# Two query heads at a time in the second block's grouped attention

## The chip, the cores and the metric

The kernel runs on one core of a Trainium2 chip. The core has five engines that run side by side and wait for one another by semaphores: TensorE (PE) for matmuls and transposes, VectorE (DVE), ScalarE (ACT), GpSimd (POOL) and SyncE (SP), which here only issues transfers from HBM. The metric is the time of one execution in microseconds (us) on the device. The time before is 2065.9 us, the median of 3 runs (2061.59 to 2067.75).

## The reference, cut to what matters

Two layers of a first block work on 256 tokens of width 1024, then comes a second block: a projection, two kinds of attention, an output projection, and a mixture of 32 experts. The change touches only the grouped attention (GQA) in the second block: 8 query heads of 64, 2 key/value heads, 256 queries against 512 keys (256 of a context, 256 of the tokens).

```python
def gqa_attention(q, k, v, q_block):          # q [1,256,8,64], k and v [1,512,2,64], q_block 128
    def block(qi):
        s = jnp.einsum('bhgqd,bkhd->bhgqk', qi, k) * scale
        p = jax.nn.softmax(s, axis=-1)
        return jnp.einsum('bhgqk,bkhd->bqhgd', p, v)
...
        lat_mix = jnp.concatenate([
            gqa_attention(qa, ka_all, va_all, Q_BLOCK),
            diff_attention(qb, kb_all, vb_all, lam, diff_subln[l], lambda_init, Q_BLOCK),
        ], axis=-1)
        x = x + gt1 * (lat_mix @ w_o[l])
        x = x + gt2 * moe_ffn(...)
```

The differential attention after it has 4 heads, each with two score matrices whose softmaxes are subtracted, and values of width 128.

## The kernel before

**Where the work stands.** The two layers take about the first 850 us, the second block's projections and attention some 190 us, routing about 75 us, the experts the rest. In the attention a list of jobs is worked through: `BJOBS` holds 16 GQA jobs, one for each query head and each tile of 128 queries, and then 8 differential jobs. Each engine's program is written out by hand as a loop over `j`, one step for each job plus one, and the engines meet only at semaphores, so a step of one engine can lie beside another step of another.

**A step on PE** (lines 759 to 775). `scores(j)` multiplies queries and keys of job j into the PSUM tile `score` (128 x 1024, two banks). A GQA job uses only one half of it, the halves in turn (`half_of`). Heads have 64 rows, so the matmul uses 64 of the array's 128 rows (line 726); `qaT` holds an even head in partitions 0 to 63 and an odd one in 64 to 127, and `kaT` holds each key head twice, in both halves. Then `values(j-1)`: four transposes of the probabilities into the one PSUM tile `flip` (line 741), half a projection unit of the later stages as filling (`bfill`, lines 691 and 644), and the product with the values, four blocks of 128 keys, into 64 partitions of `mixed` (line 751). Every matmul in plain fp32 is two MATMUL records in the trace; a transpose is one. After that, where a projection unit that needs turning is complete, `turn(u)` transposes it, through the same `flip` (line 701).

**What is filled in.** The units of `BUNITS` from number 6 on are the projections qb (2), kb (4), vb (4) and four pieces of `ada`; `BHALVES` says how many halves each step computes: four in step 0, then one in each of the 24 steps. `BDONE_IN[s]` lists the units that are complete in step s; DVE or ACT takes them out of their bank there or one step on, and qb and kb are turned in the next step.

**ACT** (lines 1029 to 1052) in step j copies `flip` of job j-1 to `turned` (line 1034), then computes the exponentials of job j from `score` to `probs`, with their sum (lines 1042 and 1045), and then evacuates units and turned units (line 1021). **DVE** (lines 1231 to 1266) takes the maximum of the scores of job j (line 1238 for GQA, 1241 for differential), evacuates the units of the step before (line 1216 and the rotation at 1175 to 1181), divides by the sum (lines 1250 and 1251), and copies `mixed` of job j-1 to `mix` (line 1264). `score_left` gives the count that PE waits for before it writes `score`: in the GQA jobs that of the job before the last one, since the halves alternate; otherwise that of the last.

**SP** issues the weights in the order of their list. A ring slot is written when the last unit that reads it is complete, so the expert tiles that follow wait for the last of the `ada` pieces and for the output projection (lines 579 to 621). From the second expert on, each tile's load waits until PE has used the same tile of the expert before (lines 600 to 611).

Of the kernel before, what the change touches and what calls it, by code (L numbers as in the profile page):

```python
# [20 lines left out]
ALU = mybir.AluOpType  # L21
ACT = mybir.ActivationFunctionType
AX = mybir.AxisListType

P = 128
# [140 lines left out]
BJOBS = [("gqa", h, t) for h in range(AHEADS) for t in range(TT)]  # L166
# [3 lines left out]
BHALVES = [4] + [1] * NBJ  # L170
# [5 lines left out]
for s_ in range(1, NBJ + 1):  # L176
    BFLIPS.append(("job", s_ - 1))
    BFLIPS += [("turn", u) for u in BDONE_IN[s_ - 1] if u in BTURNED]
# [34 lines left out]
def build(nc, c_in, xT, ctxT, consts, layer_params, block_params, w_in, w_uq, w_ukv, w_out_a, w_out_b, w_out_c,  # L213
          w_o, w_ada, w_qkv, w_o2, e_in, eb_in, e_out, eb_out, out, sizes=None, debug=None):
    PER = sizes or CHAINED
    with ExitStack() as ctx:
# [351 lines left out]
        def half_of(j):  # L568
            return j % 2 if BJOBS[j][0] == "gqa" else 0

# [84 lines left out]
        def block_tensor(pe):  # L655
# [63 lines left out]
            def scores(j):  # L719
                kind, hd, t = BJOBS[j]  # L720
                pe.wait_ge(score_free, score_left(S_JOBS + j))
                cols = slice(t * P, (t + 1) * P)
                if kind == "gqa":
                    lo = HALF * (hd % 2)
                    o = score[:, W * half_of(j):W * half_of(j) + W]
                    ins = pe.matmul(o, qaT[lo:lo + HALF, hd // 2, cols], kaT[lo:lo + HALF, hd // 4, :],  # L726
                                    start=True, stop=True)
                else:
                    for cp in range(2):
                        lo = HALF * cp  # L730
                        ins = pe.matmul(score[:, W * cp:W * cp + W], qbT[lo:lo + HALF, hd, cols],
                                        kbT[lo:lo + HALF, hd, :], start=True, stop=True)
                ins.then_inc(scored, 1)

            def values(j):
                kind, hd, t = BJOBS[j]
                pe.wait_ge(bprobs, j + 1)
                f = FLIP0 + BFLIPS.index(("job", j))
                pe.wait_ge(flip_free, f + 1)
                for i in range(4):  # L740
                    ins = pe.transpose(flip[:, i * P:(i + 1) * P], probs[:, j % 2, i * P:(i + 1) * P], ident)
                ins.then_inc(flipped, 1)
                bfill()
                pe.wait_ge(flip_free, f + 2)
                pe.wait_ge(mixed_free, MIXED0 + j + 1)
                for i in range(4):
                    pt = turned[:, j % 2, i * P:(i + 1) * P]
                    if kind == "gqa":
                        lo = HALF * (hd % 2)
                        kv = hd // 4  # L750
                        ins = pe.matmul(mixed[lo:lo + HALF, 0:P], va[:, i, kv * HALF:(kv + 1) * HALF], pt,  # L751
                                        start=i == 0, stop=i == 3)
                    else:
                        ins = pe.matmul(mixed[:, 0:P], vb[:, i, hd * P:(hd + 1) * P], pt, start=i == 0, stop=i == 3)
                ins.then_inc(mixed_done, 1)
# [3 lines left out]
            for j in range(NBJ + 1):  # L759
                if j < NBJ:  # L760
                    if j == 2 * AHEADS:
# [4 lines left out]
                if j == 2 * AHEADS + 1:  # L766
# [215 lines left out]
        def block_scalar(act):  # L982
# [46 lines left out]
            for j in range(NBJ + 1):  # L1029
                if j > 0:  # L1030
                    act.wait_ge(flipped, FLIP0 + BFLIPS.index(("job", j - 1)) + 1)
                    if j >= 3:
                        act.wait_ge(mixed_done, MIXED0 + j - 2)
                    act.activation(turned[:, (j - 1) % 2, :], flip[:, :], ACT.Copy).then_inc(flip_free, 1)
                if j < NBJ:
                    kind = BJOBS[j][0]
                    act.wait_ge(bmasked, j + 1)
                    if j >= 2:
                        act.wait_ge(flipped, FLIP0 + BFLIPS.index(("job", j - 2)) + 1)
                    st = stat[:, j % 2, :]  # L1040
                    a = W * half_of(j)
                    ins = act.activation(probs[:, j % 2, 0:W], score[:, a:a + W], ACT.Exp, bias=st[:, 2:3],
                                         accum_out=st[:, 4:5])
                    if kind == "diff":
                        ins = act.activation(probs[:, j % 2, W:2 * W], score[:, W:2 * W], ACT.Exp, bias=st[:, 3:4],
                                             accum_out=st[:, 5:6])
                    ins.then_inc(score_free, 1)
# [67 lines left out]
        def block_vector(dve, link, steps, base):  # L1115
# [115 lines left out]
            for j in range(NBJ + 1):  # L1231
                if j < NBJ:
# [3 lines left out]
                    a = W * half_of(j)  # L1236
                    if kind == "gqa":
                        link(dve.tensor_reduce(st[:, 0:1], score[:, a:a + W], AX.X, ALU.max))
                        dve.tensor_scalar(st[:, 2:3], st[:, 0:1], -1.0, None, ALU.mult).then_inc(bmasked, 1)
                    else:  # L1240
                        link(dve.tensor_reduce(st[:, 0:2], score[:, :].rearrange("p (a n) -> p a n", a=2), AX.X, ALU.max))
                        dve.tensor_scalar(st[:, 2:4], st[:, 0:2], -1.0, None, ALU.mult).then_inc(bmasked, 1)
                for u in BDONE_IN[j - 1] if j else ():
                    evacuate_block(u)
                if j < NBJ:
                    kind, hd, t = BJOBS[j]
                    pr, st = probs[:, j % 2, :], stat[:, j % 2, :]
                    dve.wait_ge(score_free, SCORE0 + S_JOBS + j + 2)
                    if kind == "gqa":
                        link(dve.reciprocal(st[:, 6:7], st[:, 4:5]))  # L1250
                        dve.tensor_scalar(pr[:, 0:W], pr[:, 0:W], st[:, 6:7], None, ALU.mult).then_inc(bprobs, 1)
                    else:
                        link(dve.reciprocal(st[:, 6:8], st[:, 4:6]))
# [4 lines left out]
                if j > 0:  # L1258
                    kind, hd, t = BJOBS[j - 1]
                    lo = HALF * (hd % 2)  # L1260
                    dve.wait_ge(mixed_done, MIXED0 + j)
                    cols = slice(t * P, (t + 1) * P)
                    if kind == "gqa":
                        dve.tensor_copy(mix[lo:lo + HALF, hd // 2, cols], mixed[lo:lo + HALF, 0:P]).then_inc(mixed_free, 1)
                    else:
                        dve.tensor_copy(mix[:, 4 + hd, cols], mixed[:, 0:P]).then_inc(mixed_free, 1)
# [1121 lines left out]
```

## Time and profile before

| what | us |
|---|---|
| median of 3 runs | 2065.9 |
| profiled execution, its own time | 2067.96 |
| profiled execution, span of the trace | 2066.1 |
| PE busy | 1931.6 (93%) |
| DVE busy / ACT busy | 766.3 / 547.8 |
| share of DMA and of PE in the chain that ended last | 32% / 57% |
| from the scores of job 1 to the end of the values of job 15 | 890.15 to 997.18 |
| the differential steps after it, to the start of the last transposes | 997.18 to 1031.33 |
| first matmul of the experts | 1116.52 |

The span is what the trace covers; the device adds 1.9 us around it. Busy shares are means over stages with different limits. The GQA stage is one where PE has no gap, the differential stage one where PE waits in each step, and the experts one where the transfers run at full rate. What the change touches must be read from the GQA stage alone.

### The profile page before, as it was taken

The numbers are of one execution on the slowest core, as the hardware profiler recorded it, in microseconds if no ns is written. First come the engines' busy times: TensorE is split into PE (matmuls) and PEld (weight loads), VectorE is DVE, ScalarE is ACT, GpSimd is POOL, SyncE is SP. The second block draws the span as 40 slices with busy tenths as digits, with TensorE's granted clock in tenths as the row PEclk, the third lists the DMA queues.
The fourth block names the chain that finished last, engine by engine and source line by source line (L and its number), as shares of the span: only waits on it lengthen the run. The fifth ranks groups of instructions, "written<-read, shape, count | busy, mean of one in ns | idle before, by whom it ended". The sixth has DMA issues, their size and how long they took to land.

```text
span 2066.1 us, 26980 instructions
## 1 busy us (share of the span) xinstructions
PE 1931.6 (93%) x10970; PEld 1215.5 (59%) x10970; DVE 766.3 (37%) x1477; ACT 547.8 (27%) x922; POOL 522.2 (25%) x220
## 2 busy tenths in 40 slices
PE   7999999989999999899888999999999999999996
PEld 6779889977798899444465344333333334333333
DVE  4784643348737533734544111111111111111112
ACT  4554455445544554112411000000000000000001
POOL 5775655767665566000000000000000000000000
PEclk9999999999999999899987999999999999999998
DMA  8554333565543335311542999999999999999994
GB/s 294 203 184 164 123 123 123 186 219 195 174 164 141 111 135 206 128 41 41 204 170 121 419 428 429 428 429 429 428 429 428 429 428 428 429 428 429 428 429 179
DMA packets 111408, 563.21 MB, mean 273 GB/s; under 512 B 4768, under 2 KB 24352, under 8 KB 86464
## 3 DMA queue, kind: packets, MB, share of 16 engines
q1 hardware_dynamic: 111328, 562.09, 68.1%
q8 instruction: 57, 0.93, 0.2%
q14 instruction: 23, 0.19, 0.0%
HBM read 561.02 MB, written 1.05 MB: 272 GB/s over the span
## 4 chain that ended last, share of the span: by engine, by line
PE 57%; DMA 32%; DVE 8%; ACT 2%; issue 1%; SPq 0%; DVEq 0%; ACTq 0%
DMA ring<-in_e_in_dram 32%; PE bank L1605 14%; PE bank L1595 10%; PE score L868 9%; PE bank L691 4%; PE bank L1572 3%; PE mixed L903 2%; PE bank L801 1%; PE mixed L1689 1%; PE flip L1672 1%; DVE ring L2174 1%; PE score L726 1%; PE score L1658 1%; PE flip L1630 1%; PE mixed L751 1%
## 5 line engine op out<-in xcount | busy, mean ns | idle before, releaser
L1981 POOL TENSOR_TENSOR w_lo<-ring,w_hi 128x1024 fp32r<-128x1024 f32 (+1 forms) x216 | 522.0, 2427 | 289.2 <-ACT w_hi L1883 288.4
L868 PE MATMUL score<-ring,space 128*64 128x512 f32 x2048 | 461.6, 595 | 46.8 <-DMA ring<-in_e_in_dram 45.8
L868 PEld LDWEIGHTS score<-ring,space 128*64 128x64 f32 x2048 | 142.3, 137 | 354.8 <-issue 245.6
L1883 ACT ACTIVATE w_hi<-ring 128x1024 fp32r<-128x1024 f32 (+1 forms) x216 | 226.4, 1049 | 222.6 <-PE bank L1605 123.6
L1605 PE MATMUL bank<-h_hi,w_hi 128*128 128x256 f32 x896 | 262.3, 293 | 0.0
L1605 PE MATMUL bank<-h_lo,w_hi 128*128 128x256 f32 x896 | 254.7, 284 | 0.0
L1605 PE MATMUL bank<-h_hi,w_lo 128*128 128x256 f32 x896 | 254.5, 284 | 0.0
L903 PE MATMUL mixed<-ring,space 128*64 128x512 f32 x1024 | 226.8, 595 | 0.0
L1084 ACT ACTIVATE space<-space 128x512 f32<-128x512 f32 x32 | 20.2, 631 | 719.7 <-DVE space L1385 719.7
L1385 DVE TENSOR_SCALAR space<-score 128x512 f32<-128x512 f32 x32 | 22.2, 694 | 432.7 <-PE score L868 432.7
L1605 PEld LDWEIGHTS bank<-h_hi,w_hi 128*128 128x128 f32 x896 | 173.3, 193 | 4.5 <-issue 4.4
L1605 PEld LDWEIGHTS bank<-h_lo,w_hi 128*128 128x128 f32 x896 | 173.1, 193 | 0.1
L1605 PEld LDWEIGHTS bank<-h_hi,w_lo 128*128 128x128 f32 x896 | 172.8, 193 | 0.0
L903 PEld LDWEIGHTS mixed<-ring,space 128*64 128x64 f32 x1024 | 70.7, 137 | 132.6 <-issue 130.6
L1595 PE MATMUL bank<-w_hi,h_hi 128*128 128x512 f32 (+1 forms) x320 | 131.3, 410 | 8.5 <-DVE h_lo L2037 8.5
L1398 DVE COPY space<-mixed 64x512 f32<-64x512 f32 x32 | 21.9, 684 | 295.6 <-PE mixed L903 295.6
L1595 PE MATMUL bank<-w_hi,h_lo 128*128 128x512 f32 (+1 forms) x320 | 125.1, 391 | 0.0
L1595 PE MATMUL bank<-w_lo,h_hi 128*128 128x512 f32 (+1 forms) x320 | 124.6, 390 | 0.0
L1595 PEld LDWEIGHTS bank<-w_hi,h_hi 128*128 128x128 f32 x320 | 61.1, 191 | 25.9 <-issue 12.8
L691 PE MATMUL bank<-ring,h 128*128 128x512 f32 (+1 forms) x160 | 68.4, 582 | 5.1 <-DVE h L1149 5.1
L1595 PEld LDWEIGHTS bank<-w_hi,h_lo 128*128 128x128 f32 x320 | 60.9, 190 | 12.0
L1595 PEld LDWEIGHTS bank<-w_lo,h_hi 128*128 128x128 f32 x320 | 61.1, 191 | 11.7 <-issue 1.0
(329 smaller groups left out, 2378.0 us busy)
## 6 DMA issues: line engine op xcount, KB each, us to landing
ring<-in_e_in_dram SPq DMA_DIRECT2D x128, 2048.0 KB, 25.2
ring<-in_e_out_dram SPq DMA_DIRECT2D x64, 2048.0 KB, 22.1
ring<-in_w_in_dram SPq DMA_DIRECT2D x42, 2048.0 KB, 7.8
ring<-in_w_ada_dram SPq DMA_DIRECT2D x16, 1024.0 KB, 5.3
ring<-in_w_o_dram SPq DMA_DIRECT2D x6, 2048.0 KB, 8.2
ring<-in_w_qkv_dram SPq DMA_DIRECT2D x4, 2048.0 KB, 10.1
ring<-in_w_ada_dram SPq DMA_DIRECT2D x4, 2048.0 KB, 8.0
ring<-in_w_out_a_dram SPq DMA_DIRECT2D x2, 2048.0 KB, 7.7
```

The lines of the kernel that those rows point to most:

```text
L691: ins = pe.matmul(b[:, 0:n], src[:, c, tt * P:(tt + 1) * P], w8[:, c, 0:n], start=c == 0, stop=c == DC - 1)
L726: ins = pe.matmul(o, qaT[lo:lo + HALF, hd // 2, cols], kaT[lo:lo + HALF, hd // 4, :], start=True, stop=True)
L751: ins = pe.matmul(mixed[lo:lo + HALF, 0:P], va[:, i, kv * HALF:(kv + 1) * HALF], pt, start=i == 0, stop=i == 3)
L868: ins = pe.matmul(score[HALF * blk:HALF * blk + HALF, which * W:(which + 1) * W], xs[:, 2 * j + r, HALF * hh:HALF * hh + HALF], wk[:, blk ...
L903: ins = pe.matmul(mixed[HALF * side:HALF * side + HALF, :], actT[:, hh, a * P + HALF * half:a * P + HALF * half + HALF], ring[:, 4 + half, ...
L1385: dve.tensor_scalar(glu[:, hh, :], score[:, 0:W], GLU_LIMIT, None, ALU.min).then_inc(glu_free, 1)
L1398: dve.tensor_copy(ys[0:HALF, hh, :], mixed[0:HALF, :])
L1572: ins = pe.matmul(b[:, i * T:(i + 1) * T], w_[:, c, m], y_[br][:, c, :], start=c == 0 and i == 0 and y_ is y_hi and w_ is hi, stop=c == 3 ...
L1595: ins = pe.matmul(b[:, 0:n], x_[:, c, t], w_[:, k % PARTS, i, 0:n], start=c == 0 and x_ is h_hi and w_ is w_hi, stop=c == DC - 1 and x_ is ...
L1605: ins = pe.matmul(b[:, half * T:(half + 1) * T], w_[:, k % PARTS, i, m:m + P], x_[:, c, :], start=c == 0 and half == 0 and x_ is h_hi and ...
L1883: act.activation(split_part(w_hi, k), raw_part(k), ACT.Copy).then_inc(hi_done, 1)
L1981: pool.tensor_tensor(split_part(w_lo, k), raw_part(k), split_part(w_hi, k), ALU.subtract).then_inc(lo_done, 1)
```

## The change

A GQA job now holds two neighbouring query heads. `BJOBS` has 8 GQA jobs (head pair, query tile) in place of 16. Their scores are written by two matmuls, one in each row half of the array, to the two halves of `score`. Their 8 blocks of probabilities go through `flip` in two rounds of four, in each of which the heads alternate (`BROUNDS`); each round has its own filling, so a GQA step computes two halves of units (`BHALVES`). The values of the two heads go to the two partition halves of `mixed` in turns, and one copy of 128 partitions takes them out. Since both halves of `score` are in use, PE waits for the exponentials of the job just before. The differential jobs are as they were.

```diff
-BJOBS = [("gqa", h, t) for h in range(AHEADS) for t in range(TT)]
+BJOBS = [("gqa", h, t) for h in range(0, AHEADS, 2) for t in range(TT)]
+NGQA = len(BJOBS)
...
-BHALVES = [4] + [1] * NBJ
+BROUNDS = [[[(w, c) for c in (2 * r, 2 * r + 1) for w in range(2)] for r in range(2)] if job[0] == "gqa" else
+           [[(0, c) for c in range(4)]] for job in BJOBS]
+BHALVES = [4] + [2] * NGQA + [1] * (NBJ - NGQA)
...
         def score_left(s):
-            s1 = s - S_JOBS
-            alone = not 1 <= s1 < 2 * AHEADS
-            return SCORE0 + s + (1 if alone else 0)
+            return SCORE0 + s + 1
...
-                if kind == "gqa":
-                    lo = HALF * (hd % 2)
-                    o = score[:, W * half_of(j):W * half_of(j) + W]
-                    ins = pe.matmul(o, qaT[lo:lo + HALF, hd // 2, cols], kaT[lo:lo + HALF, hd // 4, :],
-                                    start=True, stop=True)
+                for w in range(2):
+                    rows = slice(HALF * w, HALF * w + HALF)
+                    if kind == "gqa":
+                        q, k = qaT[rows, hd // 2, cols], kaT[rows, hd // 4, :]
...
+                    ins = pe.matmul(score[:, W * w:W * w + W], q, k, start=True, stop=True)
...
+                pe.wait_ge(mixed_free, MIXED0 + j + 1)
+                for r, blocks in enumerate(BROUNDS[j]):
+                    pe.wait_ge(flip_free, job_flip(j, r) + 1)
+                    for i, (w, c) in enumerate(blocks):
+                        ins = pe.transpose(flip[:, i * P:(i + 1) * P], probs[:, j % 2, w * W + c * P:w * W + (c + 1) * P],
+                                           ident)
+                    ins.then_inc(flipped, 1)
+                    bfill()
+                    pe.wait_ge(flip_free, job_flip(j, r) + 2)
+                    pt = turned[:, (BFIRST_ROUND[j] + r) % 2, :]
+                    for i, (w, c) in enumerate(blocks):
+                        if kind == "gqa":
+                            kv = hd // 4
+                            o, v = mixed[HALF * w:HALF * w + HALF, 0:P], va[:, c, kv * HALF:(kv + 1) * HALF]
+                        else:
+                            o, v = mixed[:, 0:P], vb[:, c, hd * P:(hd + 1) * P]
+                        ins = pe.matmul(o, v, pt[:, i * P:(i + 1) * P], start=c == 0, stop=c == 3)
...
                 if j > 0:
-                    act.wait_ge(flipped, FLIP0 + BFLIPS.index(("job", j - 1)) + 1)
-                    if j >= 3:
-                        act.wait_ge(mixed_done, MIXED0 + j - 2)
-                    act.activation(turned[:, (j - 1) % 2, :], flip[:, :], ACT.Copy).then_inc(flip_free, 1)
+                    if j >= 2:
+                        act.wait_ge(mixed_done, MIXED0 + j - 1)
+                    for r in range(len(BROUNDS[j - 1])):
+                        act.wait_ge(flipped, job_flip(j - 1, r) + 1)
+                        act.activation(turned[:, (BFIRST_ROUND[j - 1] + r) % 2, :], flip[:, :], ACT.Copy
+                                       ).then_inc(flip_free, 1)
...
+                    for w in range(2):
+                        ins = act.activation(probs[:, j % 2, w * W:(w + 1) * W], score[:, w * W:(w + 1) * W], ACT.Exp,
+                                             bias=st[:, 2 + w:3 + w], accum_out=st[:, 4 + w:5 + w])
...
+                    link(dve.reciprocal(st[:, 6:8], st[:, 4:6]))
                     if kind == "gqa":
-                        link(dve.reciprocal(st[:, 6:7], st[:, 4:5]))
-                        dve.tensor_scalar(pr[:, 0:W], pr[:, 0:W], st[:, 6:7], None, ALU.mult).then_inc(bprobs, 1)
+                        dve.tensor_scalar(pr[:, 0:W], pr[:, 0:W], st[:, 6:7], None, ALU.mult)
+                        dve.tensor_scalar(pr[:, W:2 * W], pr[:, W:2 * W], st[:, 7:8], None, ALU.mult).then_inc(bprobs, 1)
...
-                        dve.tensor_copy(mix[lo:lo + HALF, hd // 2, cols], mixed[lo:lo + HALF, 0:P]).then_inc(mixed_free, 1)
+                    dve.tensor_copy(mix[:, at, t * P:(t + 1) * P], mixed[:, 0:P]).then_inc(mixed_free, 1)
```

On PE, two steps of the program before (scores, transposes, half a unit of filling, values, each twice; the first has the turning of a kb unit behind it) stand as follows. A row with x3 is the rest of four.

```order
L726 MATMUL score<-space 128x512 [waits score_free]
L741 MATMUL flip<-cst,space 128x128 [waits flip_free,bprobs]
L741 MATMUL flip<-cst,space 128x128 x3
L691 MATMUL bank<-ring,space 128x512 [waits bank_free1,landed3]
L691 MATMUL bank<-ring,space 128x512 x3
L751 MATMUL mixed<-space 64x128 [waits mixed_free,flip_free]
L751 MATMUL mixed<-space 64x128 x3
L701 MATMUL flip<-cst,space 128x128 [waits flip_free,bqn_ready]
L701 MATMUL flip<-cst,space 128x128 x3
L726 MATMUL score<-space 128x512 [waits score_free]
```

One step of the changed program does the work of two: a second score matmul, then two rounds.

```order
L733 MATMUL score<-space 128x512 [waits score_free]
L733 MATMUL score<-space 128x512
L743 MATMUL flip<-cst,space 128x128 [waits flip_free,mixed_free,bprobs]
L743 MATMUL flip<-cst,space 128x128 x3
L695 MATMUL bank<-ring,space 128x512 [waits bank_free1,landed3]
L695 MATMUL bank<-ring,space 128x512 x3
L755 MATMUL mixed<-space 64x128 [waits flip_free]
L755 MATMUL mixed<-space 64x128 x3
L743 MATMUL flip<-cst,space 128x128 [waits flip_free]
L743 MATMUL flip<-cst,space 128x128 x3
L695 MATMUL bank<-ring,space 128x512 x4
L755 MATMUL mixed<-space 64x128 [waits flip_free]
```

The wait for `mixed_free` has moved from the values to the transposes ahead of them, and the two score matmuls stand side by side. On ACT, in the same part of the program before, each copy of `flip` (line 1034) is followed by the exponentials of one head.

```order
L1034 ACTIVATE space<-flip 128x512 [waits mixed_done,flipped]
L1042 ACTIVATE space<-score,space 128x512 [waits flipped,bmasked]
L1034 ACTIVATE space<-flip 128x512 [waits mixed_done,flipped]
L1042 ACTIVATE space<-score,space 128x512 [waits flipped,bmasked]
L1021 ACTIVATE space<-flip 128x4x128 [waits flipped]
```

In the changed program ACT has both copies of `flip` first, then both heads' exponentials.

```order
L1036 ACTIVATE space<-flip 128x512 [waits flipped,mixed_done]
L1036 ACTIVATE space<-flip 128x512 [waits flipped]
L1044 ACTIVATE space<-score,space 128x512 [waits flipped,bmasked]
L1044 ACTIVATE space<-score,space 128x512
L1022 ACTIVATE space<-flip 128x4x128 [waits flipped]
```

So the exponentials of job j have moved behind the second copy of job j-1.

## Rows read from the trace of the kernel before

**Rows 1.** Busy time by stretch: us, engines (instructions), granted PE clock, DMA share, GB/s.

```profile
890.15:901.00 10.85, 7.79 (x32) 4.10 (x31) 8.77 (x31) 1.87 (x4) 0.00 (x0) 0.92 0.56 193
901.00:909.51 8.51, 8.51 (x23) 4.03 (x22) 1.50 (x4) 1.87 (x4) 0.00 (x0) 0.70 0.00 0
909.51:991.08 81.57, 81.57 (x303) 40.31 (x303) 31.38 (x93) 20.68 (x46) 0.00 (x0) 1.00 0.08 27
997.18:1031.33 34.15, 27.02 (x169) 12.92 (x169) 21.68 (x50) 15.79 (x38) 0.00 (x0) 1.00 0.82 308
```

**Rows 2.** Timeline, PE, a GQA step: start, us, line, operation.

```profile
960.61 1.12 PE L726 MATMUL score<-space 64*128 64x512 f32 x2
961.67 0.66 PE L741 MATMUL flip<-cst,space 128*128 128x128 f32 x4
962.16 3.60 PE L691 MATMUL bank<-ring,space 128*128 128x512 f32 x8
965.69 1.09 PE L751 MATMUL mixed<-space 128*64 128x128 f32 x8
966.71 1.12 PE L726 MATMUL score<-space 64*128 64x512 f32 x2
```

**Rows 3.** Timeline, PE, first differential scores.

```profile
991.08 1.13 PE L731 MATMUL score<-space 64*128 64x512 f32 x4
992.14 0.66 PE L741 MATMUL flip<-cst,space 128*128 128x128 f32 x4
```

**Rows 4.** Timeline, PE, layer attention: values, then transposes.

```profile
352.08 0.66 PE L1689 MATMUL mixed<-space 128*64 128x128 f32 x8
352.67 0.66 PE L1672 MATMUL flip<-cst,space 128*128 128x128 f32 x4
```

**Rows 5.** Timeline, PE, steps 1 and 2.

```profile
896.24 0.66 PE L701 MATMUL flip<-cst,space 128*128 128x128 f32 x4
899.96 1.11 PE L701 MATMUL flip<-cst,space 128*128 128x128 f32 x4 [3.06 <-DVEq L1227]
901.00 2.07 PE L726 MATMUL score<-space 64*128 64x512 f32 x2
```

**Rows 6.** Timeline, PE, a later step with a turned unit.

```profile
915.62 0.65 PE L701 MATMUL flip<-cst,space 128*128 128x128 f32 x4
916.20 1.12 PE L726 MATMUL score<-space 64*128 64x512 f32 x2
```

**Rows 7.** Timeline, DVE and ACT, in step 1 (qb1 begins with the copy at 896.09).

```profile
891.31 0.69 DVE L1238 TENSOR_REDUCE space<-score 128x1 f32<-128x512 f32 x1 [15.01 <-PE score L726]
896.09 0.69 DVE L1216 COPY space<-bank 128x512 f32<-128x512 f32 x1 [0.23 <-DVE space L1181]
896.93 0.60 ACT L1021 ACTIVATE space<-flip 128x512 f32<-128x512 f32 x1 [3.77 <-PE flip L701]
899.99 0.16 DVE L1250 RECIPROCAL space<-space 128x1 f32<-128x1 f32 x1 [0.15 <-DVE space L1181]
900.19 0.49 DVE L1251 TENSOR_SCALAR space<-space 128x512 f32<-128x512 f32 x1
```

**Rows 8.** Timeline, all engines, a differential step.

```profile
998.36 1.23 DVE L1241 TENSOR_REDUCE space<-score 128x2 f32<-128x1024 f32 x1 [0.78 <-PE score L731]
999.82 0.69 ACT L1042 ACTIVATE space<-score,space 128x512 f32<-128x512 f32 x1 [0.29 <-DVE space L1242]
1001.30 0.17 DVE L1253 RECIPROCAL space<-space 128x2 f32<-128x2 f32 x1 [1.52 <-ACT space L1045]
1002.89 0.28 DVE L1266 COPY space<-mixed 128x128 f32<-128x128 f32 x1
1003.02 0.66 PE L741 MATMUL flip<-cst,space 128*128 128x128 f32 x4 [0.57 <-DVE space L1256]
```

**Rows 9.** Busy time by stretch, the end of the routing.

```profile
1100.00:1116.00 16.00, 14.28 (x52) 11.55 (x52) 14.01 (x37) 1.02 (x2) 0.00 (x0) 0.55 0.00 1
```

**Rows 10.** Timeline, SP, loads of expert tiles.

```profile
1120.42 12.34 SPq L598 DMA_DIRECT2D ring<-in_e_in_dram  x4
```

More of the change, by code:

```diff
@@ L165 @@
 AHEADS, DIFFS = 8, 4
-BJOBS = [("gqa", h, t) for h in range(AHEADS) for t in range(TT)]
+BJOBS = [("gqa", h, t) for h in range(0, AHEADS, 2) for t in range(TT)]
+NGQA = len(BJOBS)
 BJOBS += [("diff", h, t) for h in range(DIFFS) for t in range(TT)]
 NBJ = len(BJOBS)
-BHALVES = [4] + [1] * NBJ
+BROUNDS = [[[(w, c) for c in (2 * r, 2 * r + 1) for w in range(2)] for r in range(2)] if job[0] == "gqa" else
+           [[(0, c) for c in range(4)]] for job in BJOBS]
+BFIRST_ROUND = [sum(map(len, BROUNDS[:j])) for j in range(NBJ + 1)]
+BHALVES = [4] + [2] * NGQA + [1] * (NBJ - NGQA)
+assert all(BHALVES[j + 1] >= len(BROUNDS[j]) for j in range(NBJ))
 assert sum(BHALVES) == 2 * (BQKV - BFIRST)
@@ L176 @@
 for s_ in range(1, NBJ + 1):
-    BFLIPS.append(("job", s_ - 1))
+    BFLIPS += [("job", s_ - 1, r) for r in range(len(BROUNDS[s_ - 1]))]
     BFLIPS += [("turn", u) for u in BDONE_IN[s_ - 1] if u in BTURNED]
@@ L562, in score_left, with job_flip @@
         def score_left(s):
-            s1 = s - S_JOBS
-            alone = not 1 <= s1 < 2 * AHEADS
-            return SCORE0 + s + (1 if alone else 0)
-        def half_of(j):
-            return j % 2 if BJOBS[j][0] == "gqa" else 0
+            return SCORE0 + s + 1
+        def job_flip(j, r):
+            return FLIP0 + BFLIPS.index(("job", j, r))
         def block_sync(sp):
@@ L722, in scores @@
                 cols = slice(t * P, (t + 1) * P)
-                if kind == "gqa":
-                    lo = HALF * (hd % 2)
-                    o = score[:, W * half_of(j):W * half_of(j) + W]
-                    ins = pe.matmul(o, qaT[lo:lo + HALF, hd // 2, cols], kaT[lo:lo + HALF, hd // 4, :],
-                                    start=True, stop=True)
[L728 to L732, printed above, removed]
+                for w in range(2):
[3 more added lines that the diff above has]
+                    else:
+                        q, k = qbT[rows, hd, cols], kbT[rows, hd, :]
+                    ins = pe.matmul(score[:, W * w:W * w + W], q, k, start=True, stop=True)
                 ins.then_inc(scored, 1)
@@ L737, in values @@
                 pe.wait_ge(bprobs, j + 1)
[L738 to L744, printed above, removed]
-                pe.wait_ge(mixed_free, MIXED0 + j + 1)
[L746 to L754, printed above, removed]
+                pe.wait_ge(mixed_free, MIXED0 + j + 1)
+                for r, blocks in enumerate(BROUNDS[j]):
[11 more added lines that the diff above has]
+                            o, v = mixed[HALF * w:HALF * w + HALF, 0:P], va[:, c, kv * HALF:(kv + 1) * HALF]
+                        else:
+                            o, v = mixed[:, 0:P], vb[:, c, hd * P:(hd + 1) * P]
+                        ins = pe.matmul(o, v, pt[:, i * P:(i + 1) * P], start=c == 0, stop=c == 3)
                 ins.then_inc(mixed_done, 1)
@@ L765, in block_tensor @@
                     scores(j)
[L766 removed]
+                if j == NGQA + 1:
                     for u in range(BADA - 4, BADA):
@@ L1235, in block_vector @@
                     dve.wait_ge(scored, SCORE0 + S_JOBS + j + 1)
[L1236 to L1242, printed above, removed]
+                    link(dve.tensor_reduce(st[:, 0:2], score[:, :].rearrange("p (a n) -> p a n", a=2), AX.X, ALU.max))
+                    dve.tensor_scalar(st[:, 2:4], st[:, 0:2], -1.0, None, ALU.mult).then_inc(bmasked, 1)
                 for u in BDONE_IN[j - 1] if j else ():
@@ L1259, in block_vector @@
                     kind, hd, t = BJOBS[j - 1]
-                    lo = HALF * (hd % 2)
                     dve.wait_ge(mixed_done, MIXED0 + j)
-                    cols = slice(t * P, (t + 1) * P)
-                    if kind == "gqa":
-                        dve.tensor_copy(mix[lo:lo + HALF, hd // 2, cols], mixed[lo:lo + HALF, 0:P]).then_inc(mixed_free, 1)
-                    else:
-                        dve.tensor_copy(mix[:, 4 + hd, cols], mixed[:, 0:P]).then_inc(mixed_free, 1)
+                    at = hd // 2 if kind == "gqa" else 4 + hd
+                    dve.tensor_copy(mix[:, at, t * P:(t + 1) * P], mixed[:, 0:P]).then_inc(mixed_free, 1)
             dve.wait_ge(scored, SCORE0 + S_SUB + 1)
```

12 lines of the change are left out of this document (2 added, 10 removed).

## The prediction

> **What bounds the kernel now.** I read the busy time by stretch first. The attention starts with scores of job 1 at 890.15 and the last GQA values end at 997.18. In the long middle, 909.51 to 991.08, PE is busy for all of 81.57 us at a granted clock of 1.00, DVE for 31.4 and ACT for 20.7 [rows 1]. So in this stage only PE's work sets the time, and anything taken off PE shortens it until another engine is late. Next I read PE's timeline there, where starts and not durations count, since matmuls overlap. A step is 6.10 us from scores to scores: 1.06 for the scores of one head (two records), 0.49 for four transposes, 3.53 for half a unit of filling, 1.02 for the values (eight records) [rows 2]. A turned unit adds 0.58 [rows 6]. The chain of waits names the same four lines and nothing else in this stage.
>
> The stage begins worse. In step 1 PE waits 3.06 us for DVE, which has to rotate two qb units, and after that its clock is low: scores that take 1.12 elsewhere are recorded with 2.07, transposes 1.11 for 0.66 [rows 2, 5], and the granted clock is 0.70 from 901.00 to 909.51 [rows 1]. That stretch holds one plain step of 6.10 in 8.51, so 2.41 is lost to the clock, and the turning at 899.96 lasts 1.04 to the next start where it takes 0.58 [rows 5, 6], another 0.46. With the wait this is 5.93 us. Check: 16 steps of 6.10 and six turnings of 0.58 are 101.1, and with 5.93 give 107.0, which is 997.18 less 890.15.
>
> **The change on PE.** The number of blocks, of filling halves and of turnings is the same, so they cost what they did. Two things shrink.
> - Scores: 16 jobs of 1.06 become 8 jobs with two matmuls in two row halves. The differential jobs do just this, and four records take 1.06 from start to start [rows 3], no more than two records do [rows 2]. This saves 8 x 1.06 = 8.5 us.
> - Values: before, eight records in one column half take 1.02. In the layers' attention eight records of the same shape, which alternate between the column halves, take 0.59 to the next transposes [rows 4]. 16 such rounds save 16 x (1.02 - 0.59) = 6.9 us.
>
> A new step is then 1.06 + 2 x (0.49 + 3.53 + 0.59) = 10.28 us against 12.20 for two old ones.
>
> **Step 1.** Today PE reaches the turning of qb1 after one half of filling. Now it does two rounds first. From 890.15: scores to 891.21, first round to 895.82, second round to 900.43, turning of qb0 to 901.0. DVE has the same rotation, started 0.54 later, because it now reduces both heads (1.23 for 0.69) [rows 7, 8]; its qb1 took from 896.09 to 899.99 [rows 7], so it is ready at about 900.5, before PE asks. The 3.06 us wait goes. What is late next is the single `flip`: the second turning needs the first one copied. From the transposes at 896.24 to the end of ACT's copy at 896.93 + 0.60 are 1.29 [rows 5, 7]; with a small semaphore delay I take 1.35 in place of 0.58, a new gap of 0.8 us. As the gap is short, I let the clock stay high and give back the 2.41 and 0.46. Gain in step 1: 5.9 - 0.8 = 5.1 us. The bounds: if the clock falls all the same, only 3.06 - 0.8 = 2.3 is left; if PE also finds DVE late by as much as now, the new gap makes it -0.8; without any gap it is 5.9. I take 5.1, since the wait and the low clock stand next to each other in the rows.
>
> **Is another engine late then?** Per step, counted from the start of the scores: the second transposes start at 5.7; ACT copies `flip` from 6.4 to 7.0, then the exponentials of both heads, which with their sums take 1.5 in the differential jobs (999.82 to 1001.30) [rows 8], to 8.5. PE wants `score` at 10.3: 1.8 to spare. DVE divides with 0.2 + 2 x 0.5 [rows 7], to 9.8; PE wants the probabilities at 10.3 + 1.06: 1.5 to spare. The tightest is the copy of `mixed`, which the transposes now wait for: values end at 10.3, the copy of 0.28 [rows 8] is done at about 10.7, needed at 11.3. It lies beside the scores, with 0.6 to spare. Behind that wait stand filling and values, so if the copy were late, its whole lateness would be PE's. Rotating a kb unit (about 4 us on DVE) lies between the reduction, done at 2.6, and the division at 8.6. Cost of all of these: nothing, and at the other end 1.9 us a step if the wait should reach the whole saving, 15.3 us.
>
> **Downstream.** The differential steps are bound by DVE, ACT and PE in turn (period 4.7, PE waiting 0.57 for probabilities in each [rows 8]; granted clock 1.00 [rows 1]), not changed, and enter with the same work done. The units come earlier, never later, in relation to the loads: the slots are freed earlier too. Routing needs the attention's result. In its last 16 us the transfers stand still (DMA share 0.00) [rows 9], since all six tiles are loaded, and the next expert load is issued at 1120.42, after the experts have begun [rows 10]. So the experts' stream of transfers, which bounds the rest, moves as a block with the attention's end.
>
> **Sum.** 8.5 + 6.9 + 5.1 = 20.5 us. The profiled execution took 2067.96 (span 2066.1 and 1.9 around it), so 2047.5; it lies 2.1 above the median of the three runs, and from the median it is 2045.4. I predict 2046.
>
> **Rivals.**
> - One pairing does not overlap. Then its term stays away: 8.5 (to 2054) or 6.9 (to 2052). For it: no row shows a GQA job with either pattern. Against: both patterns are in the trace, with the same shapes [rows 3, 4], the scores in two banks in each case. The Trainium skill, "TensorEngine Tiling (Array Packing)", Gotcha 1 (PSUM Pressure), says that different row tiles can't use one PSUM bank at the same time; were that so for column tiles, which do share the bank of `mixed`, the values would be the pairing that fails. The trace disagrees: 0.59 in one bank of `mixed` [rows 4].
> - ACT's order takes the saving back. The exponentials of job j now stand behind the second copy of job j-1, and `score` has no second half to write meanwhile. If PE waits about 1.9 us per step, 15.3 are gone and only step 1's 5.1 is left: 2061. Against it stands the 1.8 us to spare above. The skill's same page, section "PSUM Bottleneck", says that tiling quickens TensorE and not the evacuation of PSUM, which may then bound. By that rule this is where it would show; the trace agrees for the differential steps, where PE waits 0.57 [rows 8].
> - Slower: the same chain wholly exposed. From the reduction at 998.36 to the transposes at 1003.02 the differential chain takes 4.66 us [rows 8], in which PE would stand still once in each of the 8 new steps, because ACT reaches the exponentials only after the last filling of the step: 8 x 4.7 = 37, less 20.5, gives +17, or 2083. It decides for slower from 20.5 / 8 = 2.6 us of waiting per step on. It would need the copies and exponentials to come 4.4 us later than I count (1.8 to spare and 2.6). A low clock would add to it, as after the 3.06 us wait.
> - It is hidden. If the experts' transfers had been waiting for something that the attention does not move, the time stays at 2066. Against: the share of 0.00 [rows 9] and the load after the start [rows 10].
> - Better than I say: routing runs at a granted clock of 0.55 in its last 16 us [rows 9], and where the clock falls may move with the work's phase, by some 3 us either way; the good side is about 2041.
>
> **Chances.** Forecast 0.76; one pairing fails 0.10; better 0.04: these are faster, 0.90. ACT's order 0.04 and hidden 0.03 lie within 0.3% (6.2 us, about what a measurement of this kernel can tell from no change): 0.07. Slower 0.03. The forecast's own range is 2042 to 2051, from the clock (3 us) and from the runs' scatter. The range for 8 in 10 reaches up into the failed pairing: 2040 to 2055.
>
> **What would show it.** In the new trace, the four score records and the next transposes stand 1.06 apart; the values take 0.59 to what follows; a step is 10.3 us; PE has no gap in GQA steps beyond one of about 0.8 before the turning of qb1, where the clock stays at 1.00; the time from the scores of job 1 to the end of the last GQA values falls from 107.0 to about 86.6; from there to the first expert matmul it stays at 119.3 within 3 us. I am wrong if score records follow each other at 0.5 us (row halves one after the other), if PE waits for exponentials or for the copy of `mixed`, if the clock is low in that stage, or if the stage shrinks and the end does not.

## The result

| | median us | runs | ratio to the kernel before |
|---|---|---|---|
| before | 2065.4 | 4 (2061.6 to 2067.8) | |
| changed | 2038.2 | 4 (2036.6 to 2042.4) | 0.9873 (0.9852 to 0.9894) |
| predicted | 2046 | range 2040 to 2055 | |

The kernel became 27.2 us faster, 1.8 us below the low end of the range. In a second comparison the gain was 23.6 us (2062.7 to 2039.1, ratio 0.9881, 0.9864 to 0.9897). The predicted 20.5 us is right for the stage that was worked out, and too small for the whole.

Busy time by stretch in the changed kernel's first trace: job 0, then everything between the stage and the experts, then the experts. Columns are as in [rows 1].

```profile
867.84:884.48 16.64, 16.64 (x36) 6.73 (x36) 2.44 (x5) 2.70 (x5) 0.00 (x0) 0.90 0.11 40
971.07:1088.93 117.86, 93.19 (x469) 65.69 (x467) 64.19 (x143) 30.23 (x58) 0.00 (x0) 0.87 0.43 164
1088.93:2036.20 947.27, 884.43 (x4320) 368.31 (x4320) 170.08 (x368) 72.33 (x118) 0.00 (x0) 1.00 0.97 413
```

The same three stretches in the first trace of the kernel before:

```profile
871.77:890.15 18.38, 18.38 (x35) 7.44 (x35) 1.50 (x4) 2.03 (x3) 0.00 (x0) 0.81 0.09 32
997.18:1116.52 119.34, 95.09 (x467) 66.61 (x467) 64.34 (x144) 30.47 (x57) 0.00 (x0) 0.86 0.42 162
1116.52:2066.10 949.58, 885.82 (x4320) 369.18 (x4320) 169.88 (x368) 72.39 (x118) 0.00 (x0) 0.99 0.97 412
```

Span by span the 29.9 us between the two traces (2066.1 and 2036.2) come out as follows. Ahead of job 0's scores 3.9 (871.77 against 867.84); job 0 itself 1.7; the GQA stage 20.4 (107.03 against 86.59, the time from 884.48 to 971.07); behind it 1.5; the experts 2.3. Only the third of these numbers, the stage, was in the prediction's sum.

Inside the stage the rows are those that it named. These are lines from the timeline of one new step of the changed kernel, those that answer to [rows 2, 3, 4 and 8]; the weight loads and some shorter operations of ACT and DVE are left out. Line numbers are those of the changed kernel: 733 is the scores, 743 the transposes, 755 the values, 705 the turning.

```profile
907.63 1.13 PE L733 MATMUL score<-space 64*128 64x512 f32 x4
908.69 0.66 PE L743 MATMUL flip<-cst,space 128*128 128x128 f32 x4
909.18 3.60 PE L695 MATMUL bank<-ring,h 128*128 128x512 f32 x8
912.71 0.66 PE L755 MATMUL mixed<-space 128*64 128x128 f32 x8
913.30 0.66 PE L743 MATMUL flip<-cst,space 128*128 128x128 f32 x4
913.79 3.60 PE L695 MATMUL bank<-ring,h 128*128 128x512 f32 x8
913.99 0.60 ACT L1036 ACTIVATE space<-flip 128x512 f32<-128x512 f32 x1 [3.95 <-PE flip L743]
915.15 0.69 ACT L1044 ACTIVATE space<-score,space 128x512 f32<-128x512 f32 x1
916.56 0.48 DVE L1246 TENSOR_SCALAR space<-space 128x512 f32<-128x512 f32 x1
917.32 0.66 PE L755 MATMUL mixed<-space 128*64 128x128 f32 x8
918.02 0.29 DVE L1256 COPY space<-mixed 128x128 f32<-128x128 f32 x1 [0.98 <-PE mixed L755]
```

The four score records and the next transposes are 1.06 apart, the values take 0.59 to what follows, PE has no gap. Counted from the scores, ACT copies the second round at 6.4, has the second head's exponentials under way at 7.5, DVE ends at 9.4 and the copy of `mixed` at 10.7, 0.6 us ahead of the next transposes, which start at 11.3 or later. In step 1 PE's timeline answers to [rows 5]:

```profile
894.77 0.66 PE L705 MATMUL flip<-cst,space 128*128 128x128 f32 x4
896.21 0.63 PE L705 MATMUL flip<-cst,space 128*128 128x128 f32 x4 [0.78 <-ACT space L1022]
896.76 1.13 PE L733 MATMUL score<-space 64*128 64x512 f32 x4
```

The 3.06 us wait for DVE is now a 0.78 us wait for ACT's copy of `flip`, and the scores after it take 1.13 and not 2.07.

### The profile page after: what moved, and what is told of

It reads as the page before. It is cut to its first block, busy times and chain, and to the rows that moved or that the text cites. A ratio compares the mean times of both kernels' runs of the same rounds, so it can differ in the third digit from the quotient of the medians.

```text
span 2036.2 us, 26901 instructions
## 1 busy us (share of the span) xinstructions
PE 1904.2 (94%) x10970; PEld 1199.2 (59%) x10970; DVE 759.7 (37%) x1445; ACT 546.9 (27%) x922; POOL 522.6 (26%) x220
## 4 chain that ended last, share of the span: by engine, by line
PE 57%; DMA 31%; DVE 7%; ACT 2%; issue 1%; SPq 0%; DVEq 0%; ACTq 0%
DMA ring<-in_e_in_dram 31%; PE bank L1595 14%; PE bank L1585 10%; PE score L869 9%; PE bank L695 4%; PE bank L1562 3%; PE mixed L904 2%; PE bank L802 1%; PE mixed L1679 1%; PE flip L1662 1%; DVE ring L2164 1%; PE score L1648 1%; PE flip L1620 1%; PE bank L927 1%; PE score L887 1%
```

## The experiments

They answer two questions: whether the three terms inside the stage have the causes that I gave, and where the rest comes from. Since the stage is the same to 0.1 us from trace to trace, I read each from there; the whole time scatters by several microseconds.

**The two kernels once more** (nothing edited).

> The kernel before, unchanged, for a second trace. The changed kernel was 27.2 us faster, the attention stage only 20.4 us shorter. If the rest is chance (low-clock stretches that fall differently from run to run in parts that the change doesn't touch): the stage from the scores of job 1 to the end of the GQA values is again 107.0 within 0.5, while the start of that stage (890.15 in the first trace) moves by some us and the ratio to the kernel before is 1.000. If the rest is systematic: the stage starts again at 890 and the parts behind it take the same times as in the first trace.

> The changed kernel, unchanged. By chance: the stage is again 86.6 long, its start moves by some us from 884.5, and the gain over the kernel before in five rounds comes nearer to 20.4 than 27.2 is. Systematic: start again at 884.5, gain again 27.

Measured: the unchanged kernel before 2062.3, ratio to itself 0.9997 (0.9988 to 1.0007); the changed one 2039.1. Busy time by stretch, first the second trace of the kernel before, cut at the same events: ahead of job 0, job 0, the stage, behind it, the experts.

```profile
0.00:866.18 866.18, 822.59 (x5772) 716.77 (x5772) 487.11 (x828) 415.67 (x685) 523.09 (x220) 0.98 0.49 171
866.18:884.60 18.42, 18.42 (x34) 7.43 (x34) 1.50 (x4) 2.03 (x3) 0.00 (x0) 0.81 0.09 33
884.60:991.65 107.05, 104.00 (x379) 51.42 (x378) 44.91 (x135) 27.03 (x60) 0.00 (x0) 0.97 0.11 40
991.65:1111.00 119.35, 95.11 (x467) 66.66 (x467) 64.38 (x144) 30.44 (x57) 0.00 (x0) 0.86 0.42 162
1111.00:2060.70 949.70, 885.76 (x4320) 369.13 (x4320) 169.98 (x368) 72.38 (x118) 0.00 (x0) 0.99 0.97 412
```

And the second trace of the changed kernel:

```profile
0.00:871.73 871.73, 828.54 (x5772) 721.18 (x5773) 485.81 (x828) 415.66 (x685) 522.00 (x220) 0.97 0.49 170
871.73:888.44 16.71, 16.71 (x37) 6.86 (x37) 2.44 (x5) 2.69 (x5) 0.00 (x0) 0.89 0.10 36
888.44:975.02 86.58, 85.80 (x378) 40.85 (x377) 37.28 (x102) 26.14 (x58) 0.00 (x0) 1.00 0.14 49
975.02:1092.84 117.82, 93.16 (x469) 65.71 (x467) 64.17 (x143) 30.23 (x58) 0.00 (x0) 0.87 0.43 164
1092.84:2042.30 949.46, 885.84 (x4320) 369.18 (x4320) 170.15 (x368) 72.37 (x118) 0.00 (x0) 0.99 0.97 412
```

Neither theory holds whole. The part ahead of job 0 is chance: one and the same program reached job 0 at 871.77 and 866.18 in one kernel, at 867.84 and 871.73 in the other, and the first trace of the kernel before was the latest of them. So are the experts, 947.3 or 949.5 in the changed kernel. But two parts that I had counted as untouched are not chance: job 0 takes 18.4 in both traces of the kernel before and 16.6 to 16.7 in both of the changed one, at a granted clock of 0.81 against 0.89 and 0.90; and the part behind the stage takes 119.3 against 117.8. With the stage that is 1.7 + 20.4 + 1.5 = 23.6 us, the gain measured in this second comparison.

**Values in other orders and halves.** In `values_apart` the blocks of a round are sorted by head.

```diff
-BROUNDS = [[[(w, c) for c in (2 * r, 2 * r + 1) for w in range(2)] for r in range(2)]
+BROUNDS = [[[(w, c) for w in range(2) for c in (2 * r, 2 * r + 1)] for r in range(2)]
```

> The changed kernel with the blocks of a round sorted by head: two blocks in one column half, then two in the other, instead of in turns. If the saving of the values comes from two column halves at work side by side, eight records take about 1.02 again instead of 0.59 (perhaps 0.1 less, where the halves meet), the stage is 16 x 0.43 = 6.9 us longer, and the time 2045. If the saving comes from anything else in the fused job, the round stays at 0.59 and the time at 2038.

Measured: 2040.7, ratio 0.9898 (0.9876 to 0.9920), stage 86.7. The eight records still take 0.59 (PE's timeline):

```profile
911.54 0.66 PE L755 MATMUL mixed<-space 128*64 128x128 f32 x8
912.13 0.66 PE L743 MATMUL flip<-cst,space 128*128 128x128 f32 x4
```

So the turns, which I took for the reason, are not needed. In this order too the trace has two records under way from the first 0.02 us of a round on, as with the blocks in turns. Whether the halves are needed, `values_one_half` asks.

```diff
-o, v = mixed[HALF * w:HALF * w + HALF, 0:P], va[:, c, kv * HALF:(kv + 1) * HALF]
+o, v = mixed[0:HALF, 0:P], va[:, c, kv * HALF:(kv + 1) * HALF]
+first, last = (c == 0 and w == 0, c == 3 and w == 1) if kind == "gqa" else (c == 0, c == 3)
```

> The changed kernel with the values of both heads in the lower column half, summed into one result (the two heads are no longer kept apart). Sorting the blocks by head cost nothing, so either two column halves work side by side whatever the order of the records, or eight short records cost 0.59 here for another reason. Two halves needed: 1.02 per round, the stage 14 x 0.43 = 6.0 us longer and the whole 16 x 0.43 = 6.9 us. Another reason: 0.59, no change.

Measured: 2046.5, ratio 0.9914 (0.9896 to 0.9931). PE's timeline:

```profile
914.42 1.09 PE L756 MATMUL mixed<-space 128*64 128x128 f32 x8
915.44 0.66 PE L743 MATMUL flip<-cst,space 128*128 128x128 f32 x4
```

1.02 a round, as in the kernel before [rows 2], and the stage 93.47 for 86.58, which is 6.9. (All 16 rounds lie in the stage as I cut it; the 14 of the expectation was a slip.) The term of 6.9 is confirmed: two column halves work side by side, in both orders that were run.

**Scores in one row half** (`scores_one_half`).

```diff
-q, k = qaT[rows, hd // 2, cols], kaT[rows, hd // 4, :]
+q, k = qaT[0:HALF, hd // 2, cols], kaT[0:HALF, hd // 4, :]
```

> The changed kernel with both score matmuls of a GQA job in the lower row half (the second head's scores are left out, the first one's are computed twice). If the saving of the scores comes from two row halves at work side by side, four records take 1.06 + 0.86 = 1.9 instead of 1.06, the stage is 8 x 0.86 = 6.9 us longer, and the time 2045. If it comes from fewer changes between tile shapes, they stay near 1.06 and the time at 2038.

Measured: 2048.8, ratio 0.9934 (0.9918 to 0.9951). PE's timeline:

```profile
910.20 1.98 PE L733 MATMUL score<-space 64*128 64x512 f32 x4
912.12 0.66 PE L743 MATMUL flip<-cst,space 128*128 128x128 f32 x4
```

1.92 for 1.06; the stage, which holds seven of the eight GQA scores, is 92.53 for 86.58, 0.85 for each. The row halves carry this term. The whole time rose by 9.7 against the changed kernel's 2039.1, more than the 6.9 expected: job 0 took 19.26 for 16.7, and the part behind the stage 119.5 for 117.8. The granted clock is low for longer at both places; the next pair tests the first of them.

**Job 0's scores and the clock.** `before_job0_pair` adds a matmul to the kernel before:

```diff
+                    if j == 0:
+                        pe.matmul(mixed[:, :], qaT[HALF:P, 0, cols], kaT[HALF:P, 0, :], start=True, stop=True)
```

> The kernel before, with one more score matmul in job 0 alone: the odd head's, in the upper row half, into the tile mixed, where nobody reads it. In two traces of the kernel before, the time from the scores of job 0 to those of job 1 is 18.4 us, in three of the changed kernel and its variant with paired scores 16.6 to 16.8, though both fill the same four halves there. Theory: with both row halves at work in job 0's scores the clock comes back sooner, so this kernel takes 16.7 there and is 1.7 us faster than the kernel before. Rival: it is chance or the fused job's later work, and the stretch stays at 18.4.

`after_job0_single` changes job 0 of the changed kernel:

```diff
+                    if kind == "gqa" and j == 0:
+                        q, k = qaT[0:HALF, hd // 2, cols], kaT[0:HALF, hd // 4, :]
```

> The changed kernel, with both score matmuls of job 0 alone in the lower row half (the second head's scores of that job are left out, the first one's are computed twice). Theory (both row halves bring the clock back sooner): from job 0's scores to job 1's the low clock lasts longer, about 19.2 us instead of 16.7, the rest of the stage stays at 86.6. Rival: only the second matmul's own time is added, 0.9 us at the high clock or 1.7 at the low one, 17.6 to 18.4.

Measured: 2060.7 (ratio 0.9987, 0.9976 to 0.9999) and 2043.5 (0.9907, 0.9887 to 0.9928). Busy time by stretch, `before_job0_pair`, job 0 and the stage:

```profile
868.70:885.35 16.65, 16.65 (x37) 6.72 (x37) 1.50 (x4) 2.03 (x3) 0.00 (x0) 0.90 0.12 43
885.35:991.13 105.78, 102.72 (x380) 50.76 (x379) 44.90 (x135) 27.04 (x60) 0.00 (x0) 0.98 0.11 40
```

`after_job0_single`, job 0:

```profile
866.34:885.61 19.27, 19.27 (x36) 7.81 (x37) 2.44 (x5) 2.69 (x5) 0.00 (x0) 0.82 0.08 31
```

One more matmul makes the kernel before shorter by 1.7 us in job 0: granted clock 0.90 where it was 0.81. In the other direction job 0 takes 19.27, at 0.82, against the theory's 19.2 and at most 18.4 for the rival. That is 0.9 more than in the kernel before: a second matmul in the same row half costs its own time and does nothing for the clock. Job 0 comes after gaps in which PE waits for ACT and DVE (2.22, 0.70 and 0.48 us in the kernel before), and its clock is low there at the start. One rival is left: `before_job0_pair` came to job 0 with the clock still high (the two transposes ahead of it took 0.41), the kernel before with the clock already low (0.66). The second traces of the two kernels settle it, since both come to job 0 with the clock low. Their job 0 cut 3.60 and 7.00 us after the start of the scores, first the kernel before:

```profile
866.18:869.78 3.60, 3.60 (x4) 1.34 (x5) 0.85 (x2) 1.82 (x2) 0.00 (x0) 0.50 0.45 167
869.78:873.18 3.40, 3.40 (x5) 1.35 (x4) 0.65 (x2) 0.20 (x2) 0.00 (x0) 0.50 0.00 0
```

Then the changed kernel:

```profile
871.73:875.33 3.60, 3.60 (x6) 1.34 (x7) 1.40 (x2) 1.26 (x2) 0.00 (x0) 0.50 0.45 166
875.33:878.73 3.40, 3.40 (x9) 1.52 (x8) 1.05 (x3) 1.43 (x4) 0.00 (x0) 1.00 0.00 0
```

With paired scores the full clock is back 3.6 us after they start, with single ones 7.0 us after; 3.4 us at half the clock cost 1.7 us, the whole difference. The other traces fall in the same two groups: 3.6 us wherever the scores of job 0 are paired, `before_job0_pair` too, and 7.0 us in `scores_one_half`, `after_job0_single` and `before_no_rotation`. That paired scores bring the clock back sooner is thus shown in both directions, for this place. The stage of `before_job0_pair` is also 1.3 shorter than 107.05, with the low clock around the 3.06 us wait shorter (the scores there are recorded with 1.52 and not 2.07); this I had not expected. The two together are the 3.0 us between the medians, 2063.7 and 2060.7, of which the interval of the ratio only just excludes nothing.

The 1.5 us behind the stage need no pairing to appear. Eleven traces, in which PE has the same instructions there, give 117.8 (the changed kernel twice, `values_apart`, `values_one_half`, and below `fill_behind` and `before_no_rotation`, which has no pairing), 119.3 to 119.5 (the kernel before twice, `before_job0_pair`, `scores_one_half`) and 121.8 (`after_job0_single`). The kernel before shows a low clock around the last differential step. PE's timeline in its second trace, whose first row follows a wait of 1.98:

```profile
1025.79 0.66 PE L741 MATMUL flip<-cst,space 128*128 128x128 f32 x4 [1.98 <-DVE space L1256]
1026.38 1.55 PE L644 MATMUL bank<-ring,silu 128*32 128x512 f32 x8
1027.86 2.08 PE L754 MATMUL mixed<-space 128*128 128x128 f32 x8
```

In the changed kernel the wait before the same transposes is 2.00, and the filling and values after it take 1.07 and 1.16:

```profile
1005.46 0.63 PE L743 MATMUL flip<-cst,space 128*128 128x128 f32 x4 [2.00 <-DVE space L1250]
1006.01 1.07 PE L648 MATMUL bank<-ring,silu 128*32 128x512 f32 x8
1007.01 1.16 PE L755 MATMUL mixed<-space 128*128 128x128 f32 x8
```

The same wait, once with the clock falling and once without, and the same way in both traces of each program. The kernel before has one stretch of low clock more there, and it makes 1.4 of the 1.5 us: from the start of this filling to PE's next matmul behind the values are 5.03 us in the kernel before (1026.38 to 1031.41) and 3.63 in the changed one (1006.01 to 1009.64). That the work ahead decides whether the clock falls is likely from this, with two traces of each, and not shown. The long low clock in job 0 is not enough for it: `before_no_rotation` has that too (18.4 us) and stays at 117.8. What is, no run isolates.

**The wait in step 1** (`before_no_rotation`, on the kernel before).

```diff
-                if xt >= 0:
+                if xt >= 0 and kind != "qb":
```

> The kernel before without the rotation of the two qb units (those queries are then not rotated). This takes away what PE waits for in step 1. By the prediction's third term the wait of 3.06 us goes, a gap of 0.8 at the single flip tile appears in its place, and the low clock after it (2.9 us) does not come: stage 107.0 - 5.1 = 101.9. Rival: the low clock comes anyway, at this place or a little later, and only 2.3 us go: 104.7.

Measured: 2054.5, ratio 0.9956 (0.9942 to 0.9970), stage 101.84. PE's timeline:

```profile
890.67 0.66 PE L701 MATMUL flip<-cst,space 128*128 128x128 f32 x4
892.11 0.63 PE L701 MATMUL flip<-cst,space 128*128 128x128 f32 x4 [0.78 <-ACT space L1021]
892.67 1.12 PE L726 MATMUL score<-space 64*128 64x512 f32 x2
```

The third term, 5.1 us, comes out as 5.2 in the kernel before, with the two rotations and so the wait taken away; the clock stays high and the gap at `flip` is the predicted one. The rival of 104.7 falls. The whole is 9.2 us shorter (2063.7 to 2054.5): 5.2 here, 1.5 behind the stage, and 2.5 that no cut places.

**What the filling between transposes and values is worth** (`fill_behind`, on the changed kernel).

```diff
-                    bfill()
+                    if r == 0:
+                        bfill()
```

> The changed kernel, with the second half unit of filling of each GQA step behind the second round's values instead of between its transposes and values. PE then has nothing to do while ACT copies flip: a wait of about 0.8 (transposes to the end of the copy are 1.35, transposes alone 0.49) in each of 8 steps, 7 us longer in all. The exponentials of the job still have the 3.5 us of filling as cover. Rival: if the clock falls with these gaps, as after the 3.06 us wait of the kernel before, the loss is several times as large.

Measured: 2046.1, ratio 0.9917 (0.9900 to 0.9933), stage 93.44, 6.9 longer. PE's timeline:

```profile
914.37 0.66 PE L743 MATMUL flip<-cst,space 128*128 128x128 f32 x4
915.71 0.66 PE L756 MATMUL mixed<-space 128*64 128x128 f32 x8 [0.69 <-ACT space L1037]
```

The second round's values start 1.34 us after the transposes, where 0.49 us are taken by the transposes themselves: 0.85 us in each of eight steps is the loss. The clock did not fall with these gaps, so the rival falls.

**A version meant to beat both.** The differential steps are still bound by DVE and ACT in turn. `diff_halves` cuts the step in two (for differential jobs):

```diff
+link(dve.tensor_reduce(st[:, 0:1], score[:, 0:W], AX.X, ALU.max))
+dve.tensor_scalar(st[:, 2:3], st[:, 0:1], -1.0, None, ALU.mult).then_inc(first_max, 1)
+link(dve.tensor_reduce(st[:, 1:2], score[:, W:2 * W], AX.X, ALU.max))
+dve.tensor_scalar(st[:, 3:4], st[:, 1:2], -1.0, None, ALU.mult).then_inc(bmasked, 1)
...
+dve.wait_ge(first_exp, j - NGQA + 1)
+link(dve.reciprocal(st[:, 6:7], st[:, 4:5]))
+link(dve.tensor_scalar(pr[:, 0:W], pr[:, 0:W], st[:, 6:7], None, ALU.mult))
```

> The changed kernel, with the differential steps cut in two on DVE and ACT: the maximum of the first score half goes to ACT before that of the second is taken, and DVE scales the first half while ACT computes the second one's exponentials. There a step is 4.72 us in the trace, DVE and ACT taking turns: reduction 1.22, exponentials 1.5, reciprocal to product 1.75, copy of mixed 0.28. If this chain is what bounds the stage, DVE's part ahead of the first exponential shrinks by 0.5 and the scaling of 0.5 goes beside ACT: period about 4.0 and 7 x 0.7 = 5 us off. Rival: more instructions with fixed costs and PE's own path (transposes, filling, values, scores, 3.4 us) eat it, period 4.5 or more and no more than 1.5 us off.

`diff_halves_mix` moves the copy of `mixed` as well:

```diff
+                    if early_copy:
+                        take_mixed()
                     dve.wait_ge(score_free, SCORE0 + S_JOBS + j + 2)
```

> As diff_halves, and DVE copies mixed of the job before between its scaling of the first half and the wait for the second exponentials, not at the end of the step. If the copy of 0.28 at the end of the step is on the chain, another 7 x 0.2 = 1.4 us go. If the values are not yet done at that point, DVE waits there for PE and the step is longer than in diff_halves.

Measured: 2037.3, ratio 0.9867 (0.9849 to 0.9884), and 2036.7, ratio 0.9876 (0.9857 to 0.9895). PE's timeline in `diff_halves`, one step:

```profile
980.40 0.63 PE L745 MATMUL flip<-cst,space 128*128 128x128 f32 x4 [0.37 <-DVE space L1269]
980.95 1.07 PE L650 MATMUL bank<-ring,silu 128*32 128x512 f32 x8
981.95 1.16 PE L757 MATMUL mixed<-space 128*128 128x128 f32 x8
983.11 1.13 PE L735 MATMUL score<-space 64*128 64x512 f32 x4
984.61 0.63 PE L745 MATMUL flip<-cst,space 128*128 128x128 f32 x4 [0.37 <-DVE space L1269]
```

The period is 4.21 for 4.72, and 31.1 us pass from the scores at the end of the stage to the last filling, where they were 34.9 (975.10 to 1006.21, and 971.07 to 1006.01). That is 3.8 of the 5 expected, between theory and rival; where the rest went is not isolated. The earlier copy gained nothing: the period is 4.24. In one step the values end at 980.30 and the copy starts at 980.41, ahead of the division that PE waits for, so PE's own values now stand in that chain. The medians lie 1.8 and 2.4 below the changed kernel's 2039.1, but the intervals of the ratios overlap: the traces show a shorter stretch, one trace each, and that either version beats the changed kernel as a whole is not shown.

## Why the prediction was wrong

**The sum's three terms were right, and right in their causes.** The stage was predicted at 86.6 and took 86.59 and 86.58. Scores in two row halves: 1.06, undone 1.92. Values in two column halves: 0.59, undone 1.02. Step 1: 5.1 predicted, 5.2 measured alone. The gap of 0.8 at `flip` is 0.78. The reason "in turns" for the values was too narrow; the halves do it.

**The rivals** of the stage fell, the slower one with them. Both pairings overlap; that two column halves may write one bank of `mixed` side by side, which I weighed against the row-tile rule of the Trainium skill ("TensorEngine Tiling (Array Packing)", Gotcha 1), held in both orders of the records. ACT's order takes nothing: in the waits of the changed stage PE stands once, for 0.8 us, and that is for the copy of `flip` in step 1. It was not hidden either. "Better than I say", with a chance of 0.04, came nearest. It had the right kind of cause, the clock falling elsewhere, but looked for it in the routing, and to either side; the routing's last 16 us have a granted clock of 0.57 and 0.58 in the two kernels.

**The step that failed** is "Downstream ... not changed, and enter with the same work done", and beside it the silence about job 0. I let the change act only from the scores of job 1 on. Job 0's scores are also paired, and this ended the low clock there sooner: 1.7 us, shown in both directions. Behind the stage one stretch of low clock is missing in the changed kernel, at the last differential step: 1.5 us, the same in each program's two traces, with its cause open. So both terms stood at nothing in the sum: the downstream one by an argument on the work, which is indeed the same, and job 0's without a word. With them the sum would have been 23.7 us in place of 20.5 and the range 2037 to 2052, which holds the measured 2038.2. "I let the clock stay high" was an argument about one wait, and the same argument had to be made for every place near the change where the granted clock is under 1: job 0 had 0.81, and the differential stage's end 0.86 with what follows. The expected check, "119.3 within 3 us", did allow for it, but as chance to both sides, not as a term.

**The rest is scatter, most of it in the base.** With 23.6 us the forecast from the median before (2065.4) would have been 2042, 3.6 us above what was measured. The remaining 3.6 of the 27.2 lie in no repeated difference: the part ahead of job 0, the same in every program, takes 866 to 872, and the experts take 947 or 949.5. Three later sets of runs of the kernel before (13, 14 and 7) have medians of 2062.7, 2063.7 and 2063.2, so the 2065.9 that the forecast started from was 2 to 3 us high. From 2062.7 the 23.6 us give 2039.1, which is what was measured beside it. A base of three runs, with a spread of 6 us, should have widened the low side by as much.

## What to carry to other kernels

Time the operation in question in another stage of the same kernel where it already runs in the new form: two numbers of this kind (1.06 and 0.59), with the step's own rows, gave a stage of 87 us to 0.1 us. Then look at every stretch with a low granted clock near the change, ahead of it too, and give the clock a term of its own, and to the range the scatter of the base. Where an evacuation lies between two PE operations, keep independent PE work between them; here each such half unit was worth 0.85 us.

## What the runs showed of the hardware

- One added matmul in the idle row half, whose result nobody read, made a program faster at that place: 18.4 to 16.65 us in job 0, granted clock 0.81 to 0.90, and 2063.7 to 2060.7 in all (ratio 0.9976 to 0.9999). The full clock was back 3.6 us after the scores' start, 7.0 us without it.
- Records sorted by column half overlap as well as alternating ones, two at a time from the start of a round: eight in 0.59 us in both orders, and 1.02 in one half. The two halves write one bank.
- A wait of 2.0 us before the same transposes was followed by a low clock in both traces of one program and in neither trace of another; the waits of 0.69 and 0.78 us in the GQA stage were not.
